# Four weight block sums formed during the first feed-forward product and kept in DRAM

## The chip, the cores and the metric

The kernel runs on one core of a Trainium2 chip. The metric is the time of one execution in microseconds (us), measured on the device. Five engines of the core matter: TensorE (PE in the profile) multiplies; VectorE (DVE), ScalarE (ACT) and GpSimd (POOL) work elementwise; SyncE (SP) issues nearly all DMA transfers, in the order in which its program lists them, and stands still where it waits for a semaphore.

## The reference, cut to what matters

The reference is two transformer blocks over 512 tokens of width 1024, all in float32. The change touches only the end of the second block:

```python
def hybrid_layer(x, ...):
    ...
    h = rms_norm_2(x, norm_mlp)
    return x + jnp.square(jax.nn.relu(h @ w_ff1)) @ w_ff2   # w_ff1 1024x4096, w_ff2 4096x1024

def second_block(x, ...):
    ...
    return rms_norm_2(x, norm_final)
```

## The kernel before

Every float32 matrix is split into a high part (the value rounded to `fp32r`) and a low part (value minus high part), and a product is three matmuls: high by high, low by high, high by low. ACT writes the high parts, DVE subtracts to get the low parts, and PE adds the three into one PSUM bank.

**First feed-forward product** (`ff_tile`). 32 output chunks `c` of 128 features by 512 tokens. A chunk takes 8 x 3 = 24 matmuls of 128x512. Its weights (`unit`, 128x1024) come from a ring `wring` whose slots hold four chunks each (groups `f1_0` to `f1_7`, 2048 KB per group). ACT copies the unit to `w_hi` (L1652) once PE is done with chunk `c - 3`, DVE makes `w_lo` (L2214), ACT applies relu and square into `ffT` (L1350, L1352). SP refills a slot once DVE has made the four low parts of its last group (`last_use`, L609). The ring has three slots.

**Second feed-forward product.** The 4096 rows of `w_ff2` are taken as 16 pairs of 128 rows. A pair is a 2x2 block matrix (two row blocks by two column halves of 512; in `pair_raw` they lie as quarters 0 to 3), and the activations of the pair are 2x2 as well (two chunks by two halves of the tokens). The kernel uses a seven-product scheme in place of eight: each product is a block or sum of blocks of the activations by a block or sum of blocks of the weights. All seven do not fit in the eight PSUM banks, so there are two sweeps over the 16 pairs: indices m = 0 to 15 form four products per pair (`first_of`, 24 matmuls), m = 16 to 31 three (`second_of`, 18 matmuls, the weights loaded a second time). Between the sweeps DVE adds the eight banks into `x` while PE works on the last two pairs.

For each m the steps are: SP loads 1024 KB of `w_ff2` into one of six places (L742; place m is free when pair m - 6 has been used by PE, semaphore `pair_used`); POOL forms the weight sums in place (`weight_sums`: L2424, 1024 wide, and L2426, 512 wide, in the first sweep; L2428 and L2429, 512 wide each, in the second), and in the first sweep one sum of activations (`side_sum`, L2418, 256 wide); DVE forms two differences of activations in the first sweep (L2236, 512 wide); ACT writes `s_hi` (L1675) and `f_hi` (L1682 to L1686); DVE writes `s_lo` (L2240, 2048 wide, in the second sweep 1536) and `f_lo` (L2243 and L2244, 256 and 768 wide; in the second sweep L2246 and L2247, 256 and 512). PE waits for `f_lo_done` before each pair. The high and low activations have four places; places 1 to 3 lie where the high and low parts of the first product's input are, so `side_sum(1)` waits until that product has ended (`a_full`, `A2_END + NF`). During the first feed-forward product POOL also adds two totals per pair to `ffT` (`side_totals`, L2409 and L2410).

At the end the last four pairs are held: product 0 of all four is finished first, then the others bank by bank, so that the final norm of the first token tiles runs beside PE.

## Time and profile before

| | us |
|---|---|
| three timed runs | 1111.55, 1111.72, 1116.86 (median 1111.72) |
| profiled execution | 1115.25 |
| its span, first to last instruction | 1113.4 |
| PE busy | 1055.2 (95%) |
| DVE busy | 696.2 (63%) |
| ACT busy | 513.8 (46%) |
| POOL busy | 316.6 (28%) |
| DMA | 121 MB, mean 109 GB/s |

Busy time is a share of the whole span and hides that the stages have different limits: the strip of the page with 40 slices shows PE at 9 tenths or more nearly everywhere up to the 32nd slice (28 us each), and 6 to 8 tenths in most of the slices after that, where the second feed-forward product runs. Matmul durations overlap in the records: a 128x512 matmul is shown as about 0.39 us and the next one starts 0.23 us after it. The granted clock says at which share of 2.4 GHz PE ran.

### The profile page before, as it was taken

The page shows a single profiled execution, that of the slowest core. Times are in us where ns is not written, and L with a number is a line of the kernel's source. Part 1 is how long each engine was busy: PE and PEld are TensorE (multiplying, and loading weights), DVE is VectorE, ACT ScalarE, POOL GpSimd, SP SyncE. Part 2 cuts the span into 40 slices and gives each one's busy share as a digit, 9 for nine tenths or more (in the row PEclk, how much of TensorE's full clock was granted, in tenths as well). Part 3 has the DMA queues.
Part 4 walks back from the last instruction along what each step waited for, and adds up shares of the span by engine and source line. Part 5 has one row for each costly group of instructions (what it writes and reads, how often), then busy time and mean ns, then how long its engine had stood idle before and what let it go on. Part 6 is the DMA issues. An engine that isn't in the chain of part 4 may idle for free. (4 is left out here: it accounts for less than half of the span.)

```text
span 1113.4 us, 14191 instructions
## 1 busy us (share of the span) xinstructions
PE 1055.2 (95%) x5364; PEld 856.9 (77%) x5364; DVE 696.2 (63%) x1156; ACT 513.8 (46%) x929; POOL 316.6 (28%) x274
## 2 busy tenths in 40 slices
PE   9999999999899999999999999999999967887896
PEld 7788888888788889877777778888888855666664
DVE  5579996666853335154678693422222389999896
ACT  8453454554642422454678642343333433444543
POOL 0021110022300018001444100011111689874971
PEclk9999999999999999999999999999999988998999
DMA  8554332324100852222004511433223213342752
GB/s 314 109 120 114 95 89 63 77 95 152 68 29 21 271 170 58 76 76 53 5 1 151 190 45 70 151 134 113 76 76 117 110 43 128 131 151 94 257 178 76
DMA packets 79283, 121.06 MB, mean 109 GB/s; under 512 B 4288, under 2 KB 41920, under 8 KB 79216
## 3 DMA queue, kind: packets, MB, share of 16 engines
q1 hardware_dynamic: 78288, 117.37, 32.5%
q0 software_dynamic: 784, 2.75, 1.7%
q8 instruction: 43, 0.70, 0.3%
q14 instruction: 24, 0.20, 0.1%
q10 hardware_dynamic: 144, 0.03, 0.0%
HBM read 115.30 MB, written 4.85 MB: 108 GB/s over the span
## 5 line engine op out<-in xcount | busy, mean ns | idle before, releaser
L1228 PE MATMUL bank<-s_hi,f_hi 128*128 128x512 f32 x224 | 95.3, 426 | 39.1 <-DVE f_lo L2244 30.4
L2214 DVE TENSOR_TENSOR w_lo<-wring,w_hi 128x1024 fp32r<-128x1024 f32 x32 | 40.6, 1267 | 122.5 <-ACT w_hi L1652 122.5
L784 PE MATMUL bank<-u_hi,h_hi 128*128 128x512 f32 (+1 forms) x288 | 110.9, 385 | 1.4 <-ACT arena L1321 1.1
L1782 DVE TENSOR_TENSOR u_lo<-wring,u_hi 128x1024 fp32r<-128x1024 f32 (+1 forms) x64 | 78.9, 1242 | 53.3 <-ACT u_hi L1394 52.7
L784 PE MATMUL bank<-u_hi,h_lo 128*128 128x512 f32 (+1 forms) x288 | 109.2, 379 | 0.0
L784 PE MATMUL bank<-u_lo,h_hi 128*128 128x512 f32 (+1 forms) x288 | 109.0, 378 | 0.0
L1394 ACT ACTIVATE u_hi<-wring 128x1024 fp32r<-128x1024 f32 (+1 forms) x64 | 65.9, 1034 | 87.0 <-PE bank L784 68.1
L784 PE MATMUL bank<-h_hi,w_lo 128*128 128x512 f32 (+2 forms) x272 | 104.5, 384 | 0.0
L784 PE MATMUL bank<-h_hi,w_hi 128*128 128x512 f32 (+2 forms) x272 | 104.4, 384 | 0.0
L784 PE MATMUL bank<-h_lo,w_hi 128*128 128x512 f32 (+2 forms) x272 | 104.3, 384 | 0.0
L784 PE MATMUL bank<-h_hi,u_hi 128*128 128x512 f32 x224 | 95.1, 424 | 0.3 <-ACT arena L1336 0.2
L1230 PE MATMUL bank<-s_lo,f_hi 128*128 128x512 f32 x224 | 92.0, 411 | 0.0
L1229 PE MATMUL bank<-s_hi,f_lo 128*128 128x512 f32 x224 | 91.9, 410 | 0.0
L2240 DVE TENSOR_TENSOR s_lo<-wring,s_hi 128x2048 fp32r<-128x2048 f32 (+1 forms) x32 | 84.6, 2645 | 9.2 <-ACT s_hi L1675 9.2
L1228 PEld LDWEIGHTS bank<-s_hi,f_hi 128*128 128x128 f32 x224 | 44.5, 199 | 59.1 <-DVE f_lo L2244 35.9
L784 PE MATMUL bank<-h_hi,u_lo 128*128 128x512 f32 x224 | 87.9, 392 | 0.0
L784 PE MATMUL bank<-h_lo,u_hi 128*128 128x512 f32 x224 | 87.6, 391 | 0.0
L2409 POOL TENSOR_TENSOR arena<-arena 128x256 f32<-128x256 f32 x16 | 11.8, 737 | 244.1 <-ACT arena L1352 244.1
L1652 ACT ACTIVATE w_hi<-wring 128x1024 fp32r<-128x1024 f32 x32 | 33.9, 1058 | 95.4 <-PE bank L784 95.4
L2395 POOL TENSOR_SCALAR arena<-arena,stats 128x128 f32<-128x128 f32 (+3 forms) x64 | 39.4, 626 | 123.7 <-DVE stats L2167 123.7
L1675 ACT ACTIVATE s_hi<-wring 128x2048 fp32r<-128x2048 f32 (+1 forms) x32 | 54.2, 1693 | 37.2 <-PE bank L1230 26.2
L784 PEld LDWEIGHTS bank<-u_hi,h_hi 128*128 128x128 f32 x288 | 54.1, 188 | 13.0 <-issue 2.9
(322 smaller groups left out, 2532.4 us busy)
## 6 DMA issues: line engine op xcount, KB each, us to landing
wring<-in_w_ff SPq DMA_DIRECT2D x32, 1024.0 KB, 4.9
wring<-in_w_in SPq DMA_DIRECT2D x60, 512.0 KB, 3.9
wring<-in_w_ff SPq DMA_DIRECT2D x8, 2048.0 KB, 8.2
arena<-in_w_out SPq DMA_DIRECT2D x4, 1024.0 KB, 5.1
wring<-in_w_out SPq DMA_DIRECT2D x2, 2048.0 KB, 12.5
arena<-in_first SPq DMA_DIRECT2D x8, 418.0 KB, 5.6
arena<-in_x SPq DMA_DIRECT2D x4, 512.0 KB, 10.5
arena<-bias_copies POOLq DMA_DIRECT2D x8, 256.0 KB, 5.9
```

The lines of the kernel that those rows point to most:

```text
L784: last = mm(b, lhs, rhs, start=(start and n == 0), stop=(stop and n == 2))
L1228: mm(b, f[0][:, token], w[0][:, high], start=start, stop=False)
L1229: mm(b, f[1][:, token], w[0][:, high], start=False, stop=False)
L1230: return mm(b, f[0][:, token], w[1][:, lows], start=False, stop=stop)
L1394: run(u_hi[u % HI_UNITS][:, 0:unit_cols(u)], raw_unit(u), ACT.Copy).then_inc(u_hi_done, 1)
L1652: run(dst, src, ACT.Copy).then_inc(w_hi_done, 1)
L1675: run(s_hi[m % 4][:, 0:PAIR - at], pair_raw(m)[:, at:PAIR], ACT.Copy).then_inc(s_hi_done, 1)
L1782: v.tensor_tensor(u_lo[u % RAW_UNITS][:, 0:cols], raw_unit(u), u_hi[u % HI_UNITS][:, 0:cols].bitcast(F32), ALU.subtract).then_inc(u_lo_don ...
L2214: v.tensor_tensor(cut(w_lo[ring3(m)]), src, cut(w_hi[ring3(m)]).bitcast(F32), ALU.subtract).then_inc(w_lo_done, 1)
L2240: v.tensor_tensor(s_lo[pair_place(m)][:, at:PAIR], pair_raw(m)[:, at:PAIR], s_hi[m % 4][:, 0:PAIR - at].bitcast(F32), ALU.subtract)
L2395: g.tensor_scalar(place, place, den2[:, u:u + 1], gates[:, i, at:at + 1], ALU.mult, ALU.mult).then_inc(scaled, 1)
L2409: g.tensor_tensor(f[:, 256:512], f[:, 256:512], f[:, 768:D], ALU.add)
```

## The change

1. **POOL and SP during the first product.** While PE runs the first feed-forward product, each pair of `w_ff2` is loaded into one of two places in the middle slot of the ring (`load_pair`), POOL forms four of the five weight sums (`pair_sums`: one instruction 1024 wide, two 512 wide), and SP writes them to a DRAM tensor `sums_kept` (`keep_sums`, two transfers of 512 KB). The next load into the place waits until that write has landed. The first-product groups `f1_2` to `f1_7` now alternate between two slots only, and their loads stand in SP's program behind rounds 0, 3, 6, 9, 12 and 14 of this loop.
2. **First sweep.** SP loads two quarters of `w_ff2` and one kept sum (three transfers of 256 KB); POOL adds one sum of 512 (`weight_sum`) and one activation sum of 256.
3. **Second sweep.** SP loads three kept sums (768 KB). POOL forms no weight sum; it forms one sum and one difference of activations, 256 wide each.
4. **Products regrouped.** The four products of the first sweep take one difference of activations from DVE (256 wide, `side_diff`) in place of two. `f_lo` is made by two instructions of 512. The adds into `x` between the sweeps are 14 in place of 12, those at the end 10 in place of 12; behind the very last product stands one add and one square in place of two and two.
5. **A place for pair 1** (index m = 1): its activations go to `wring` 0 to 2047, which is also place 0 of the weight ring. `side_sum(1)` waits for `w_lo_done` 32 in place of the end of the first product. The load for m = 4, which uses that same place, waits for `pair_used` 2. In DVE's program `side_diff(m + 1)` now stands ahead of `lows(m)`.

```diff
+    sums_kept = nc.dram_tensor("sums_kept", (NP, P, PAIR), F32).ap()
...
+        f_at = (("arena", 26720), ("hT", 0), ("hT", 2 * D), ("arena", 24672), ("wring", 0))
+        f_place = lambda m: 4 if m == 1 else m % 4
+        sum_raw = lambda j: wring[:, SLOT + PAIR * (j % 2):SLOT + PAIR * (j % 2 + 1)]
+        sum_out = [wring[:, 12288:12288 + D], arena[:, 26720:26720 + D]]
...
         def slot(name, width=512):
-            s = number[name] % RING
+            s = (2, 0)[int(name[3:]) % 2] if name[0] == "f" else number[name] % RING
...
+            def load_pair(j):
+                if j < 2:
+                    sp.wait_ge(*last_use("w2o1"))
+                else:
+                    sp.wait_ge(sums_out, 32 * (j - 1))
+                rows = w["w_ff2_2"][2 * P * j:2 * P * (j + 1), :]
+                sp.dma_start(sum_raw(j).rearrange("p (k n) -> p k n", k=2), rows.rearrange("(k p) n -> p k n", p=P)).then_inc(piece_in[6 + j % 2], 16)
+
+            def keep_sums(j):
+                sp.wait_ge(w_summed, 3 * j + 3)
+                sp.dma_start(sums_kept[j][:, 0:D], sum_out[j % 2]).then_inc(sums_out, 16)
+                sp.dma_start(sums_kept[j][:, D:PAIR], sum_raw(j)[:, S:S + D]).then_inc(sums_out, 16)
...
+            for j in range(NP):
+                keep_sums(j)
+                if j + 2 < NP:
+                    load_pair(j + 2)
+                if j in (0, 3, 6, 9, 12, 14):
+                    n = 2 + (0, 3, 6, 9, 12, 14).index(j)
+                    sp.wait_ge(w_lo_done, 4 * (n - 1))
...
+            sp.wait_ge(sums_out, 32 * NP)
             for m in range(2 * NP):
-                if m < PAIR_PLACES:
+                if 2 <= m < PAIR_PLACES:
                     sp.wait_ge(w_lo_done, 4 * (6 + m // 2))
+                if m == 4:
+                    sp.wait_ge(pair_used, 2)
+                if m >= PAIR_PLACES:
+                    sp.wait_ge(pair_used, m - PAIR_PLACES + 1)
...
+            def side_diff(m):
+                dve.wait_ge(side_sum_done, m + 1)
+                total = f_sum[f_place(m)]
+                v.tensor_tensor(total[:, 768:D], ff_pair(m)[:, 256:512], total[:, 512:768], ALU.subtract).then_inc(side_diff_done, 1)
...
-            for m in range(NP + 2):
+            side_diff(0)
+            side_diff(1)
+            lows(0)
+            lows(1)
+            side_diff(2)
+            for m in range(2, NP + 2):
+                if m + 1 < NP:
+                    side_diff(m + 1)
                 lows(m)
...
+            def pair_sums(j):
+                pool.wait_ge(piece_in[6 + j % 2], 16 * (j // 2 + 2))
+                raw = sum_raw(j).rearrange("p (q n) -> p q n", q=4)
+                g.tensor_tensor(sum_out[j % 2].rearrange("p (q n) -> p q n", q=2), raw[:, 1:3, :], raw[:, 0:4:3, :], ALU.add).then_inc(w_summed, 1)
+                pool.wait_ge(w_summed, 3 * j + 1)
+                g.tensor_tensor(raw[:, 1, :], raw[:, 1, :], raw[:, 3, :], ALU.subtract).then_inc(w_summed, 1)
+                g.tensor_tensor(raw[:, 2, :], raw[:, 2, :], raw[:, 0, :], ALU.subtract).then_inc(w_summed, 1)
+
+            def weight_sum(m):
+                pair_arrived(pool, m)
+                raw = pair_raw(m)
+                g.tensor_tensor(raw[:, 3 * S:PAIR], raw[:, 0:S], raw[:, S:2 * S], ALU.add).then_inc(w_summed, 1)
...
             def side_sum(m):
-                if m >= 4:
+                if m == 1:
+                    pool.wait_ge(w_lo_done, NF)
+                elif m >= 4:
                     pool.wait_ge(pair_used, m - 3)
...
+            for m in range(4, NP):
+                weight_sum(m)
+                side_sum(m)
+            for m in range(NP, 2 * NP):
+                side_sum(m)
```

SP's program around the two feed-forward products, before (`in_w_ff_2 128x8x512` is a group of `w_ff1`, `128x2x1024` a pair of `w_ff2`):

```order
L653 DMA wring<-in_w_branch_pool 128x4x128
L697 DMA wring<-in_w_ff_2 128x8x512 x4
L735 DMA arena<-in_norm_final 128x1024
L697 DMA wring<-in_w_ff_2 128x8x512 x4
L742 DMA wring<-in_w_ff_2 128x2x1024 x32
```

The same place in the changed program (rounds 0 to 2 of the 16):

```order
L702 DMA wring<-in_w_ff_2 128x8x512 x2
L745 DMA wring<-in_w_ff_2 128x2x1024 x2
L749 DMA sums_kept<-wring 128x1024
L750 DMA sums_kept<-wring 128x1024
L745 DMA wring<-in_w_ff_2 128x2x1024
L762 DMA wring<-in_w_ff_2 128x8x512
L749 DMA sums_kept<-arena 128x1024
L750 DMA sums_kept<-wring 128x1024
L745 DMA wring<-in_w_ff_2 128x2x1024
L749 DMA sums_kept<-wring 128x1024
L750 DMA sums_kept<-wring 128x1024
L745 DMA wring<-in_w_ff_2 128x2x1024
```

Each round is two writes and one load (L749, L750, L745). The load of group `f1_2` (L762), which followed straight on `f1_1` before, now stands behind the writes of round 0 and the load for pair 2; `f1_3` stands at the same place of round 3.

DVE's program near the start of the second product, before, for m = 2 (`s_lo4`) and m = 3 (`s_lo5`), four instructions for each:

```order
L2236 TENSOR_TENSOR hT<-arena,hT 128x512 [waits side_sum_done]
L2240 TENSOR_TENSOR s_lo4_134<-wring,s_hi2_128 128x2048 [waits s_hi_done]
L2243 TENSOR_TENSOR f_lo2_142<-arena,f_hi2_138 128x256 [waits f_hi_done]
L2244 TENSOR_TENSOR f_lo2_142<-hT,f_hi2_138 128x768
L2236 TENSOR_TENSOR arena<-arena 128x512 [waits side_sum_done]
L2240 TENSOR_TENSOR s_lo5_135<-wring,s_hi3_129 128x2048 [waits s_hi_done]
L2243 TENSOR_TENSOR f_lo3_143<-arena,f_hi3_139 128x256 [waits f_hi_done]
L2244 TENSOR_TENSOR f_lo3_143<-arena,f_hi3_139 128x768
```

The same place in the changed program:

```order
L2280 TENSOR_TENSOR hT<-arena,hT 128x256 [waits side_sum_done]
L2280 TENSOR_TENSOR arena<-arena 128x256 [waits side_sum_done]
L2287 TENSOR_TENSOR s_lo4_134<-wring,s_hi2_128 128x2048 [waits s_hi_done]
L2290 TENSOR_TENSOR f_lo2_143<-arena,f_hi2_138 128x512 [waits f_hi_done]
L2291 TENSOR_TENSOR f_lo2_143<-hT,f_hi2_138 128x512
L2280 TENSOR_TENSOR wring<-arena,wring 128x256 [waits side_sum_done]
L2287 TENSOR_TENSOR s_lo5_135<-wring,s_hi3_129 128x2048 [waits s_hi_done]
L2290 TENSOR_TENSOR f_lo3_144<-arena,f_hi3_139 128x512 [waits f_hi_done]
L2291 TENSOR_TENSOR f_lo3_144<-arena,f_hi3_139 128x512
```

The difference for m = 3 (L2280, the second row) stands ahead of the low parts for m = 2, and the one for m = 4 (`wring<-arena,wring`, the sixth row) ahead of those for m = 3; each waits for POOL's activation sum of its own m.

POOL's program at the same place, before, for m = 2 to 5 (`piece_in4` says that the pair m = 2 has landed, `piece_in0` m = 4):

```order
L2424 TENSOR_TENSOR wring<-wring 128x1024 [waits piece_in4]
L2426 TENSOR_TENSOR wring<-wring 128x512 [waits w_summed]
L2409 TENSOR_TENSOR arena<-arena 128x256 [waits a_free]
L2410 TENSOR_TENSOR arena<-arena 128x256
L2418 TENSOR_TENSOR hT<-arena 128x256 [waits a_full]
L2424 TENSOR_TENSOR wring<-wring 128x1024 [waits piece_in5]
L2426 TENSOR_TENSOR wring<-wring 128x512 [waits w_summed]
L2418 TENSOR_TENSOR hT<-arena 128x256 [waits a_full]
L2424 TENSOR_TENSOR wring<-wring 128x1024 [waits piece_in0]
L2426 TENSOR_TENSOR wring<-wring 128x512 [waits w_summed]
L2418 TENSOR_TENSOR arena<-arena 128x256 [waits a_full]
L2424 TENSOR_TENSOR wring<-wring 128x1024 [waits piece_in1]
```

And in the changed program (L2475 is `weight_sum`, L2486 `side_sum`):

```order
L2475 TENSOR_TENSOR wring<-wring 128x512 [waits piece_in4]
L2475 TENSOR_TENSOR wring<-wring 128x512 [waits piece_in5]
L2486 TENSOR_TENSOR hT<-arena 128x256 [waits a_full]
L2461 TENSOR_TENSOR arena<-arena 128x256 [waits a_free]
L2462 TENSOR_TENSOR arena<-arena 128x256
L2486 TENSOR_TENSOR arena<-arena 128x256 [waits a_full]
L2475 TENSOR_TENSOR wring<-wring 128x512 [waits piece_in0]
L2486 TENSOR_TENSOR wring<-arena 128x256 [waits pair_used]
L2475 TENSOR_TENSOR wring<-wring 128x512 [waits piece_in1]
L2486 TENSOR_TENSOR hT<-arena 128x256 [waits pair_used]
```

The activation sum for m = 4 (`waits pair_used`, eighth row) stands behind the weight sum for m = 4, which waits for the load of that pair (`piece_in0`).

## Rows read from the trace of the kernel before

**Rows 1.** Windows: per stretch, busy us (instructions) of each engine, clock, DMA share, GB/s.

```profile
727.00:894.00 167.00, 167.00 (x725) 135.13 (x725) 43.31 (x33) 68.69 (x93) 36.03 (x37) 1.00 0.29 104
894.00:1018.00 124.00, 93.63 (x350) 71.32 (x349) 119.42 (x61) 48.20 (x52) 101.37 (x51) 0.88 0.36 119
1018.00:1106.00 88.00, 79.24 (x329) 60.65 (x327) 79.68 (x77) 38.55 (x59) 50.40 (x27) 1.00 0.43 150
```

**Rows 2.** Waits of PE from 892 to 1107: us in total, times, longest.

```profile
PE bank L1228 <- DVE f_lo L2244: 30.4, 12, 8.0
PE bank L1228 <- DVE f_lo L2247: 8.8, 10, 1.4
```

**Rows 3.** One source line, L1228: duration ns, first and last start in us.

```profile
L1228 PE MATMUL bank<-s_hi,f_hi x224: 389/397/797, 894.9 to 1105.4; 128*128 128x512 f32 x112
```

**Rows 4.** Timeline of PE within one pair: start us, us, engine, line.

```profile
1003.45 0.39 PE L1229 MATMUL bank<-s_hi,f_lo 128*128 128x512 f32 x1
...
1008.57 0.40 PE L1230 MATMUL bank<-s_lo,f_hi 128*128 128x512 f32 x1
```

**Rows 5.** Timeline of DVE over one pair beside POOL and one alone.

```profile
984.96 2.28 DVE L2240 TENSOR_TENSOR s_lo<-wring,s_hi 128x2048 fp32r<-128x2048 f32 x1
...
992.82 2.28 DVE L2240 TENSOR_TENSOR s_lo<-wring,s_hi 128x2048 fp32r<-128x2048 f32 x1
995.02 0.41 DVE L2243 TENSOR_TENSOR f_lo<-arena,f_hi 128x256 fp32r<-128x256 f32 x1
995.36 0.94 DVE L2244 TENSOR_TENSOR f_lo<-wring,f_hi 128x768 fp32r<-128x768 f32 x1
996.23 0.68 DVE L2236 TENSOR_TENSOR hT<-arena,hT 128x512 f32<-128x512 f32 x1
996.83 3.38 DVE L2240 TENSOR_TENSOR s_lo<-wring,s_hi 128x2048 fp32r<-128x2048 f32 x1
```

**Rows 6.** Timeline of POOL: three instructions with DVE idle, then those beside the pair.

```profile
864.71 0.73 POOL L2410 TENSOR_TENSOR arena<-arena 128x256 f32<-128x256 f32 x1
865.40 2.40 POOL L2424 TENSOR_TENSOR wring<-wring 128x1024 f32<-128x1024 f32 x1
867.88 1.30 POOL L2426 TENSOR_TENSOR wring<-wring 128x512 f32<-128x512 f32 x1
...
985.91 3.58 POOL L2424 TENSOR_TENSOR wring<-wring 128x1024 f32<-128x1024 f32 x1 [1.43 <-DMA wring<-in_w_ff]
989.57 1.36 POOL L2426 TENSOR_TENSOR wring<-wring 128x512 f32<-128x512 f32 x1
991.43 0.92 POOL L2418 TENSOR_TENSOR hT<-arena 128x256 f32<-128x256 f32 x1 [0.49 <-PE bank L1230]
```

**Rows 7.** Timeline of DVE in the first feed-forward product, two chunks in a row.

```profile
751.39 1.23 DVE L2214 TENSOR_TENSOR w_lo<-wring,w_hi 128x1024 fp32r<-128x1024 f32 x1 [4.41 <-ACT w_hi L1652]
756.89 1.23 DVE L2214 TENSOR_TENSOR w_lo<-wring,w_hi 128x1024 fp32r<-128x1024 f32 x1 [4.28 <-ACT w_hi L1652]
```

**Rows 8.** Timeline of SP: the loads of groups `f1_1` and `f1_2` (x2, merged).

```profile
706.87 6.82 SPq L697 DMA_DIRECT2D wring<-in_w_ff  x2
```

**Rows 9.** Landing of the two 1024 KB loads issued at 836.2 and 836.6.

```profile
L742 SPq DMA_DIRECT2D wring<-in_w_ff x2: 367/418/469, 836.2 to 836.6; - x2
DMA to landing us min/median/max: 4.7/5.8/6.8
```

**Rows 10.** Page, DMA issues: the writes of the output, 256 KB each.

```profile
out<-x SPq DMA_DIRECT2D x8, 256.0 KB, 2.0
```

**Rows 11.** Windows around DMA transfers and around PE's longest wait, columns as in rows 1.

```profile
836.00:844.00 8.00, 8.00 (x36) 6.49 (x35) 1.35 (x2) 2.19 (x4) 1.43 (x2) 1.00 0.71 262
1107.00:1113.00 6.00, 0.00 (x0) 0.00 (x0) 2.28 (x5) 2.19 (x7) 2.49 (x2) 0.82 0.58 219
...
907.00:910.00 3.00, 1.35 (x3) 1.16 (x4) 3.00 (x2) 0.00 (x0) 2.92 (x3) 0.50 0.00 0
910.00:913.00 3.00, 3.00 (x9) 2.28 (x8) 3.00 (x3) 2.63 (x3) 3.00 (x2) 0.52 0.00 0
```

**Rows 12.** Chain that ended last, its end: start us, us, what.

```profile
1106.27 1.29 DVE x L2254 x2
1107.56 0.02 issue
1107.58 0.94 ACT junk L1706 x3
```

## What was predicted

> **What bounds the kernel now.** I read the windows by stage first, then the waits of PE, then PE, DVE and POOL on the timeline, and the transfers last. In the first feed-forward product PE is busy in all of 727 to 894, while DVE works 43 of 167 us, POOL 36 and the DMA engines 0.29 of the time [rows 1]. In the second product, 894 to 1106, it is the other way round: DVE is busy 119.4 of 124 us in the first sweep and 79.7 of 88 in the rest, POOL 101 and 50, and PE has gaps [rows 1]. All of PE's waits there are for DVE's last instruction of a pair, `f_lo`, 39.2 us in 22 waits, the longest 8.0 [rows 2]. The granted clock is 0.88 in the first of the two stretches [rows 1]: the gaps also cost speed behind them.
>
> What PE would need: from the second to the last matmul of a pair, 22 steps, 5.12 us pass, 0.2327 us a matmul [rows 4]. A first-sweep pair of 24 is 5.58 us, a second-sweep pair of 18 is 4.19, and all 3 x 224 = 672 [rows 3] are 156.4 us. They took from 894.9 to 1106.2 [rows 3, 12], 211.3 us. So 54.9 us lie between this stage and a dense PE.
>
> What DVE needs: alone it starts the instructions of a pair 2.20 (2048 wide), 0.34 (256), 0.87 (768) and 0.60 us (512) apart, 4.01 us for the four (992.82 to 996.83) [rows 5]. One pair earlier, beside POOL, the same four took 992.82 - 984.96 = 7.86 us [rows 5]. In that time POOL did three instructions that alone take 2.48, 1.26 and 0.70 us, 4.44 in sum [rows 6] (865.40 to the next start, 867.88, and 0.03 to 0.04 less than the shown length for the other two). The extra 3.85 us is 0.87 of POOL's own work. So a pair costs DVE its own time plus 0.87 times what POOL does meanwhile: 4.01 + 0.87 x 4.44 = 7.9 us against PE's 5.58. DVE is the bound of the sweeps, and POOL's work is half the reason.
>
> **The sweeps, part by part.** First sweep, POOL per pair: the 1024-wide sum goes, 512 and 256 wide stay, 1.96 us in place of 4.44. DVE: 2.20 + one difference of 256 (0.34) + 2 x 0.60 = 3.74 in place of 4.01. Together 3.74 + 0.87 x 1.96 = 5.45 us, just under PE's 5.58. Second sweep: POOL has 2 x 0.70 = 1.40 in place of two sums of 512 (2.52); DVE is unchanged, an estimate of 1.65 for the 1536-wide low part (three quarters of 2.20) + 0.34 + 0.60 = 2.6. Together 3.8 us against PE's 4.19 (before: 4.8). In both sweeps PE becomes the bound, by a hair in the first.
>
> Here a rule speaks against the change. The Trainium skill (SBUF — State Buffer, "SBUF: two separate sides") says that DVE and GpSimd share a port pair under an exclusive lock, held for the whole instruction, the other side fully blocked. By it the two simply add up, 3.74 + 1.96 = 5.70 us, and the first sweep stays DVE-bound by 0.12 us a pair, 2 us in all. This trace has them a little better than additive: 4.01 + 4.44 = 8.45 by the rule, 7.86 measured [rows 5, 6].
>
> What PE then still loses. (a) m = 3. Pair 1 now lies in `wring` 0 to 2047, so the load for m = 4 is issued when PE has used pair 1, 2 x 5.58 = 11.2 us into the sweep (m = 0 and 1 can both be ready at its start: the activations of m = 1 no longer wait for the end of the first product, which was the 8.0 us wait). In POOL's program the activation sum of m = 4 stands behind the weight sum of m = 4, and in DVE's the difference of m = 4 stands ahead of the low parts of m = 3. So the chain is: issue 11.2; 768 KB land after 3/4 of 2.85 (below) + 1.6 + 0.5 for three issues = 4.2, 15.4; POOL 1.26 + 0.70, 17.4; DVE 0.34 + 2.20 + 1.20, 21.1; beside it POOL does the sums of m = 5, + 0.87 x 1.96 = 22.8. PE wants m = 3 at 16.7. A stall of 6.1 us. Nothing else queues long behind it: m = 4 follows 5.45 later. (b) The clock behind it. After the 8.0 us gap PE started at 908.65 and ran at half clock until about 912.9 (1.35 us busy of 907 to 910, clock 0.52 in 910 to 913) [rows 11], 2.1 us lost; I take 2. (c) Where DVE has 0.1 us of slack per pair, hiccups remain: bounds 0 and 0.4 us for each of the 16 pairs, I take 4 us for this, the sweep boundary (DVE adds 14 x 0.6 = 8.4 us there, PE has two pairs = 8.4 us in hand) and the four held pairs. Sum: 156.4 + 6.1 + 2 + 4 = 168.5 us in place of 211.3: **-42.8**.
>
> **Tail.** Behind the last product stood two adds (1.29 us) and two squares (0.94 us shown to the second's start of reading) [rows 12]; one add and one square stay: -0.6 and about -0.5. **-1.1**.
>
> **The first product: the new work.** POOL gets 16 x (2.48 + 2 x 1.26) = 80 us on an engine that has 131 idle [rows 1]; DVE's `w_lo` may take 1 us longer each, and has 4.3 us of idle ahead of it [rows 7]. Both are hidden. The DMA queue is another matter. 1024 KB move in 2.85 us (0.71 of 8 us for 2048 KB), written at the same rate (0.58 of 6 us at 219 GB/s, which is 1.31 MB) [rows 11]; two loads issued 0.4 us apart landed 4.7 and 6.8 us after their issues, that is one after the other, with 7.2 - 5.7 = 1.5, I take 1.6 us beside the moving [rows 9]. SP does one round per pair: write the sums, wait until they have landed, load the pair after next, next round. The write of a round stands behind the load of the one before, so a round is 2.85 + 2.85 + 1.6 + 0.3 for semaphores = 7.6 us (POOL's 5.0 + 1.4 fit in). Every third round also has a `w_ff1` group in front of the write, + 5.7 = 13.3. Three rounds are 28.5 us, with the write waiting a little for POOL 28.8. PE eats a group of four chunks in 4 x 24 x 0.2327 = 22.3 us [rows 4] (one chunk from 751.39 to 756.89 [rows 7]). Supply is slower than use, the ring is one slot shorter, and what counts is how long the head start lasts:
> - the first pair loads are issued at 713.3 (706.87 + 6.82 - 0.37) [rows 8], land 718, summed 723.5, written 728, then load and group: `f1_2` is there at 739.5;
> - `f1_6` is four triples later, 739.5 + 115.2 = 854.7. Its first chunk (24) starts in PE eight chunks, 8 x 5.58 = 44.6 us, before the end of the product (894.4, half a microsecond ahead of the first start in [rows 3]), at 849.8, and ACT and DVE need 2.4 us: wanted at 847.4. **7.3 us late**. `f1_5` is 0.8 late, `f1_7` (two rounds later) arrives at 871, wanted at 869.7 + 7.3, in time. So PE waits at chunks 20 and 24, 7.3 us together, and about 1.5 us of half clock behind: **+8.8**.
> The loads of the sweeps start when all sums are out, about 874, and m = 0 is wanted near the end of the product: hidden.
>
> The Trainium skill (DMA: Bandwidth & Descriptors, "Anatomy of one DMA") puts a fixed 2.0 us on a transfer, most of it the receipt of the last write, longest where the target is HBM, and every round here waits for just that. The output writes give 2.0 - 0.7 = 1.3 us for it [rows 10, 11]. With the page's 2.0 a round would be 0.4 us longer, 12 rounds lie before `f1_6`, and the sum would be 4.8 us higher.
>
> **The sum.** -42.8 - 1.1 + 8.8 = -35.1 us, against the profiled execution of 1115.25 (span 1113.4 and 1.85 around it): 1080.2. That execution lies 3.5 us above the median of the timed runs; I carry the difference over and forecast 1111.7 - 35.1 = **1077 us**.
>
> **The rivals.**
> - *The rounds keep up.* If a group may overtake or the fixed part is nearer 1.3, `f1_6` comes in time and the first product stays whole: 8.8 less, 1068. For it: PE's slack is only missed by 7 in 115 us. Against it: it needs all triples at 27 us or less.
> - *Longer rounds.* One microsecond more per round (POOL slowed by DVE, a slower receipt, the write not right behind the load) comes 12 times: 1089. For it: a chain of waits across SP, DMA and POOL seldom runs without gaps; before, such a wait of SP did not exist in this stage.
> - *The rounds starve the first product* (the other side). Place: PE at chunks 16, 20 and 24, waiting for `w_hi`. The saving of 43.9 is eaten when `f1_6` is 44 us late less the clock, which is 12 rounds of 10.6 in place of 7.6 and up: writes to DRAM at less than half the rate of reads. With 3.5 us more per round, 1119. Against it: the output writes move at the rate of reads [rows 11].
> - *DVE stays the bound.* If what an instruction of DVE loses is a fixed 1.1 us (3.38 against 2.28 [rows 5]) whenever POOL is active at all, not a share of POOL's work, a first-sweep pair costs 3.74 + 4 x 1.1 = 8.1 and the sweep gains nothing: 1077 + 16 x 2.5 = 1117 and more. Against it: POOL will be idle two thirds of each pair, and the pair at 992.82 shows no loss while POOL idles.
>
> **Chances.** Forecast, 1072 to 1083: 0.47. Rounds keep up, 1064 to 1072: 0.20. Longer rounds or larger rests in the sweeps, 1083 to 1102: 0.24. The two last: 0.03 and 0.02, and 0.04 for something in between that leaves no change. Faster 0.91, same 0.04, slower 0.05, where within 0.5% (5.6 us) a measurement can't tell a change from none. Range 1060 to 1099: both ends reach past the neighbouring cases, since the length of a round enters twelvefold.
>
> **What would show it.** In the windows of the changed kernel: DVE's share in the first sweep still near 1 but a pair in 5.6 us; PE's waits for `f_lo` down from 39 to about 10, of them one of 6 us at m = 3, 16 to 17 us into the sweep; writes of sums spaced 7.6 and 13.3 us; two waits of PE on `w_lo` at chunks 20 and 24, 1 and 6.5 us; POOL near 116 us busy in the first product. The forecast is wrong if PE waits in the first product at chunk 16 already or not at all, or if DVE takes over 6 us a pair in the first sweep.

## The result: 1.5% faster, less than half of the forecast gain

| | before | changed |
|---|---|---|
| median of 4 timed runs each, us | 1112.84 | 1096.54 (1095.39 to 1097.95) |
| ratio | | 0.985, 95% interval 0.982 to 0.988 |
| span of the profiled execution, us | 1113.4 | 1096.1 |
| second product: first and last start of its first line | 894.9, 1105.4 | 920.3, 1088.1 |

16.3 us were gained where 35.1 were forecast. The second product is as short as forecast; it begins 25.4 us later than before, where 8.8 were forecast.

Windows of the changed kernel, the first product and then the second, columns as in [rows 1]:

```profile
727.00:920.00 193.00, 176.47 (x735) 141.61 (x735) 51.77 (x35) 70.17 (x97) 113.12 (x81) 0.95 0.71 244
920.00:1089.00 169.00, 159.78 (x675) 127.81 (x673) 136.85 (x140) 89.18 (x112) 67.78 (x62) 0.97 0.39 134
```

PE now has 16.5 us of gaps in the first product, which was gapless [rows 1], and POOL works 113 us there in place of 36 (over 193 us in place of 167). In the second, DVE is busy 81% of the stretch; in [rows 1] it was 94% over the two. PE's waits from 700 to 1097 (total, times, longest), and the line that answers to [rows 3]:

```profile
PE bank L826 <- ACT arena L1394: 16.5, 3, 6.0
PE bank L1270 <- DVE f_lo L2291: 9.0, 1, 9.0
...
L1270 PE MATMUL bank<-s_hi,f_hi x224: 389/396/792, 920.3 to 1088.1; 128*128 128x512 f32 x112
```

Of the 22 waits for `f_lo` [rows 2] one is left. The 16.5 us are new, and they are not waits for `w_lo` but for ACT's square (L1394), which releases a PSUM bank.

SP's timeline over one triple of rounds, that is three rounds of which the first has a group in front of its writes (L745 loads a pair, L749 and L750 write its sums, L762 loads a group of `w_ff1`):

```profile
728.24 0.38 SPq L745 DMA_DIRECT2D wring<-in_w_ff  x1
728.67 0.52 SPq L762 DMA_DIRECT2D wring<-in_w_ff  x1
731.07 0.34 SPq L749 DMA_DIRECT2D sums_kept<-arena  x1
...
741.57 0.38 SPq L745 DMA_DIRECT2D wring<-in_w_ff  x1
...
751.75 0.38 SPq L745 DMA_DIRECT2D wring<-in_w_ff  x1
...
760.19 0.38 SPq L745 DMA_DIRECT2D wring<-in_w_ff  x1
760.62 0.47 SPq L762 DMA_DIRECT2D wring<-in_w_ff  x1
```

Rounds of 13.3, 10.2 and 8.4 us, where 13.3, 7.6 and 7.6 were forecast. The next groups are issued at 792.4, 824.0, 855.2 and 869.5: over the four triples 31.6 us each and not 28.8. Windows show the rate, first over a round with a group (three quarters of its bytes are reads) and then in stretches of three such triples where a load and a write follow each other alone:

```profile
728.50:741.50 13.00, 13.00 (x59) 10.58 (x58) 4.05 (x4) 5.90 (x8) 8.34 (x5) 1.00 0.89 323
742.00:748.00 6.00, 6.00 (x28) 4.84 (x27) 1.49 (x2) 2.33 (x4) 0.01 (x1) 1.00 0.81 242
774.00:780.00 6.00, 6.00 (x28) 4.84 (x27) 1.23 (x1) 2.66 (x5) 1.06 (x1) 1.00 0.86 249
805.90:812.00 6.10, 6.10 (x16) 4.76 (x17) 1.23 (x1) 1.83 (x3) 0.00 (x0) 0.55 0.77 207
```

Divided by the share of time in which the DMA engines were busy: 323 / 0.89 = 363 GB/s in the first, then 299, 290 and 269. [rows 11] gave 262 / 0.71 = 369 for reads alone and 219 / 0.58 = 378 for writes alone: neither shows the two together.

ACT's timeline where `f1_6` lands, then the SP line L762 as a whole, who waits for it and how long its transfers take:

```profile
865.55 1.06 ACT L1694 ACTIVATE w_hi<-wring 128x1024 fp32r<-128x1024 f32 x1 [12.59 <-DMA wring<-in_w_ff]
866.51 0.58 ACT L1392 ACTIVATE arena<-bank 128x512 f32<-128x512 f32 x1
867.12 0.63 ACT L1394 ACTIVATE arena<-arena 128x512 f32<-128x512 f32 x1
```

```profile
L762 SPq DMA_DIRECT2D wring<-in_w_ff x6: 469/471/870, 728.7 to 869.5; - x6
...
  ACT w_hi L1694: 36.4, 3
DMA to landing us min/median/max: 10.3/10.7/13.8
```

In ACT's program the copy of chunk c + 3 (L1694) stands ahead of the relu and square of chunk c (L1392, L1394). When a group is late, ACT stands at its first unit (chunk c + 3), and the bank of chunk c, which PE has finished, stays full. PE has two banks for this product, so it can still work on c + 1 and is stopped before c + 2: one chunk, 5.58 us, before it would need the late weights.

### The profile page after: what moved, and what is told of

It is laid out like the page before. It is cut to its first block and busy times, and to the rows that moved or that the text cites. A ratio compares the mean times of both kernels' runs of the same rounds, so it can differ in the third digit from the quotient of the medians.

```text
span 1096.1 us, 14319 instructions
## 1 busy us (share of the span) xinstructions
PE 1051.2 (96%) x5364; PEld 858.7 (78%) x5364; DVE 644.7 (59%) x1156; ACT 515.6 (47%) x929; POOL 318.2 (29%) x306
## 5 line engine op out<-in xcount | busy, mean ns | idle before, releaser
L2261 DVE TENSOR_TENSOR w_lo<-wring,w_hi 128x1024 fp32r<-128x1024 f32 x32 | 48.4, 1513 | 137.1 <-ACT w_hi L1694 137.1
L826 PE MATMUL bank<-h_hi,w_hi 128*128 128x512 f32 (+2 forms) x272 | 108.0, 397 | 16.9 <-ACT arena L1394 16.5
L826 PE MATMUL bank<-h_lo,w_hi 128*128 128x512 f32 (+2 forms) x272 | 107.2, 394 | 0.0
L826 PE MATMUL bank<-h_hi,w_lo 128*128 128x512 f32 (+2 forms) x272 | 107.1, 394 | 0.0
L1270 PE MATMUL bank<-s_hi,f_hi 128*128 128x512 f32 x224 | 89.7, 400 | 9.1 <-DVE f_lo L2291 9.0
L1694 ACT ACTIVATE w_hi<-wring 128x1024 fp32r<-128x1024 f32 x32 | 33.8, 1057 | 121.0 <-PE bank L826 84.6
L1271 PE MATMUL bank<-s_hi,f_lo 128*128 128x512 f32 x224 | 89.5, 400 | 0.0
L1272 PE MATMUL bank<-s_lo,f_hi 128*128 128x512 f32 x224 | 89.0, 398 | 0.0
L2287 DVE TENSOR_TENSOR s_lo<-wring,s_hi 128x2048 fp32r<-128x2048 f32 (+1 forms) x32 | 68.5, 2141 | 14.3 <-ACT s_hi L1720 14.3
L826 PEld LDWEIGHTS bank<-h_hi,w_hi 128*128 128x128 f32 x272 | 53.0, 195 | 29.6 <-ACT arena L1394 17.8
L826 PEld LDWEIGHTS bank<-u_lo,h_hi 128*128 128x128 f32 x288 | 54.1, 188 | 10.1
```

Source lines behind the costliest of these rows:

```text
L826: last = mm(b, lhs, rhs, start=(start and n == 0), stop=(stop and n == 2))
L1270: mm(b, f[0][:, token], w[0][:, high], start=start, stop=False)
L1271: mm(b, f[1][:, token], w[0][:, high], start=False, stop=False)
L1272: return mm(b, f[0][:, token], w[1][:, lows], start=False, stop=stop)
L1694: run(dst, src, ACT.Copy).then_inc(w_hi_done, 1)
L2261: v.tensor_tensor(cut(w_lo[ring3(m)]), src, cut(w_hi[ring3(m)]).bitcast(F32), ALU.subtract).then_inc(w_lo_done, 1)
```

## The experiments

The ratios of e1 to e12 are to runs of the kernel before on the chip of that experiment, medians 1114.7 to 1115.7 us; the ratio of the changed kernel is to the 1112.8 us of the first table. Spans and starts are of one execution each. "Start" and "last" are the first and last start of the second product's first line (`bank<-s_hi,f_hi`, x224) in the profiled execution.

| kernel | start | last | difference | span | median | ratio (95%) |
|---|---|---|---|---|---|---|
| changed | 920.3 | 1088.1 | 167.8 | 1096.1 | 1096.5 | 0.985 (0.982 to 0.988) |
| e1_takefirst | 911.9 | 1078.3 | 166.4 | 1086.4 | 1088.5 | 0.977 (0.975 to 0.980) |
| e2_early | 908.3 | 1076.3 | 168.0 | 1084.4 | 1086.9 | 0.976 (0.974 to 0.979) |
| e3_sidefirst | 920.2 | 1085.4 | 165.2 | 1093.5 | 1093.6 | 0.981 (0.979 to 0.983) |
| e4_reads | 913.2 | 1078.9 | 165.7 | 1086.9 | 1087.5 | 0.976 (0.973 to 0.978) |
| e5_place5 | 919.7 | 1076.5 | 156.8 | 1084.6 | 1085.7 | 0.974 (0.972 to 0.976) |
| e6_joined | 902.8 | 1064.8 | 162.0 | 1072.8 | 1075.1 | 0.964 (0.963 to 0.966) |
| e7_double | 916.6 | 1091.6 | 175.0 | 1099.1 | 1103.1 | 0.990 (0.987 to 0.992) |
| e8_oldplace | 919.7 | 1079.1 | 159.4 | 1087.2 | 1088.3 | 0.976 (0.974 to 0.978) |
| e9_split | 913.2 | 1080.9 | 167.7 | 1089.0 | 1091.3 | 0.979 (0.975 to 0.982) |
| e10_all | 901.1 | 1064.1 | 163.0 | 1072.2 | 1070.3 | 0.960 (0.957 to 0.964) |
| e11_all2 | 895.7 | 1057.1 | 161.4 | 1065.2 | 1068.6 | 0.960 (0.957 to 0.962) |
| e12_split2 | 912.5 | 1079.0 | 166.5 | 1087.1 | 1088.8 | 0.977 (0.975 to 0.980) |

**ACT's order (e1_takefirst).**

```diff
+                take(("ff", c))
                 if c + 3 < NF:
                     unit_hi(c + 3)
-                take(("ff", c))
```

> ScalarE's order in the first product is turned round: take(c) (relu and square of chunk c) stands ahead of unit_hi(c + 3), the copy that waits for the group from DMA. Theory A, the deadline: in the changed kernel ScalarE stands at unit_hi(4n) waiting for the group, take(4n - 3) stands behind it, and PE finds no free bank for chunk 4n - 1, so the group is wanted one chunk (5.58 us) earlier than its weights are used. Then PE's waits become waits for w_lo, and the second product starts 5.6 us earlier (914.7 in place of 920.3), the time falls by 5 to 6 us. Rival: the lateness is only that of the group against its first use; then turning the order changes nothing (within 1 us).

Its waits of PE, 700 to 1100:

```profile
PE bank L826 <- DVE w_lo L2261: 12.6, 2, 6.6
```

Three waits for ACT have become two for `w_lo`, the releaser and the number that the prediction had, at 6.0 and 6.6 us and not 1 and 6.5. The second product starts 8.4 us sooner, more than the 5.6 expected: `f1_6` was also issued 2.2 us sooner here (853.0 against 855.2). The span is 9.7 us shorter, since the sweeps took 1.4 us less as well. The prediction had put the deadline of a group one chunk too late.

How far a start moves by itself: e3, e5, e7 and e8 leave the loads, POOL's sums and PE's matmuls of the first product as in the changed kernel and start at 920.2, 919.7, 916.6 and 919.7. So a difference of under 4 us between two starts shows nothing by itself.

**The groups sooner (e2_early).**

```diff
-                if j in (0, 3, 6, 9, 12, 14):
+                if j in (0, 2, 4, 6, 8, 10):
```

> The groups f1_2 to f1_7 are loaded behind rounds 0, 2, 4, 6, 8 and 10 in place of 0, 3, 6, 9, 12 and 14; everything else as in the changed kernel. If the whole stretch of the first product (25.4 us) is the supply of the groups, PE is dense there again, the second product starts at 894 to 896, and what is late next is the round of pair 15: the sums are still out at about 886, the loads for m = 0 land at 891, and PE waits 3 to 8 us for its first pair. Time lower by 18 to 22 us. Rival: the DMA queue is full anyway, groups that come earlier push the writes back, the sums end later (895 or more) and half of the gain goes: 8 to 12 us.

PE no longer waits for weights in the first product, yet the second starts only 12 us earlier. PE's wait and DVE's timeline there:

```profile
908.35 0.77 PE L1270 MATMUL bank<-s_hi,f_hi 128*128 128x512 f32 x1 [12.41 <-DVE f_lo L2291]
```

```profile
896.91 0.43 DVE L2280 TENSOR_TENSOR wring<-arena,wring 128x256 f32<-128x256 f32 x1 [14.27 <-POOL wring L2486]
901.19 0.94 DVE L2280 TENSOR_TENSOR wring<-arena,wring 128x256 f32<-128x256 f32 x1 [3.85 <-POOL wring L2486]
902.05 2.81 DVE L2287 TENSOR_TENSOR s_lo<-wring,s_hi 128x2048 fp32r<-128x2048 f32 x1
```

The loads of the sweeps start when the last sums have landed, 889.0 here (885.8 in the changed kernel). The wait for weights had covered a second one, for the sums. The 11.7 us of span lie in the range of the rival (8 to 12) and not in the 18 to 22 expected: PE is dense as expected, the sums end 3 us later, not 10, and the wait for the first pair is 12.4 us, not 3 to 8. The difference for m = 1, which waits 3.85 us for POOL, stands ahead of the low parts of m = 0 and adds to it.

**Reads in place of writes (e4_reads).**

```diff
-                sp.dma_start(sums_kept[j][:, 0:D], sum_out[j % 2]).then_inc(sums_out, 16)
+                sp.dma_start(sum_out[j % 2], w["w_ff2_2"][2 * P * j:2 * P * j + P, :]).then_inc(sums_out, 16)
```

> The two writes of sums to DRAM per round are replaced by two loads of the same size (512 KB each) from w_ff2 into the same places of SBUF, and the loads of kept sums in the sweeps by loads of w_ff2 of the same size: same bytes, same order, same waits, but no DMA write to DRAM (the products then use other weights). Theory B, mixed directions: reads and writes in one queue together move at about 290 GB/s where reads alone move at 350, so a triple of rounds takes 31.6 us in place of 28.8; then without writes the triple is 28 to 29 us and the time falls by 9 to 12 us. Rival C, latency: the rounds are long because of fixed parts of waiting and issuing; then the triple stays at 31 to 32 us and the time stays within 2 us.

The second write of a round is replaced in the same way, and in the sweeps the loads of kept sums are loads of `w_ff2` of the same size; the kernel leaves out the keeping of the sums and multiplies by other weights.

The groups are issued at 728.6, 758.1, 788.9, 818.8 and 848.0: 29.85 us a triple. So 1.75 of the 2.8 us that a triple was too long belong to the writing to DRAM. The time met its number (9.2 us of span, 9 to 12 expected), the triple did not (28 to 29 expected): a part of the excess has another cause. A window of it beside that of 742 to 748 above:

```profile
743.00:749.00 6.00, 6.00 (x28) 4.84 (x27) 1.23 (x1) 2.18 (x3) 1.81 (x1) 1.00 0.82 329
```

329 / 0.82 = 401 GB/s against 299, with a load in the place of each write. The edit takes away two things at once, the slower moving and the landing of a write in DRAM. The end of this round, where the last bytes have moved and SP still waits, in the changed kernel and then in e4:

```profile
750.00:752.00 2.00, 2.00 (x10) 1.64 (x9) 0.00 (x0) 0.85 (x1) 1.92 (x3) 1.00 0.04 16
748.00:750.00 2.00, 2.00 (x10) 1.64 (x9) 0.00 (x0) 0.00 (x0) 1.92 (x2) 1.00 0.04 14
```

The DMA engines stand still for about as long in both (the next load is issued at 751.75 and 749.63), so in this round it is the moving that got longer; other rounds were not compared in this way.

**Place and order in the sweeps (e3_sidefirst, e5_place5, e8_oldplace).** e3 puts POOL's activation sum of m = 4 ahead of its weight sum; e5 moves pair 1 to place 1, so that the load for m = 5 waits and not that for m = 4, and puts the activation sums of 4 and 5 first; e8 undoes the place for pair 1, in all engines' programs, and puts `lows(0)` ahead of `side_diff(1)` in DVE's.

```diff
 # e3
-            for m in range(4, NP):
-                weight_sum(m)
-                side_sum(m)
+            side_sum(4)
+            weight_sum(4)
 # e5
-        ..., ("wring", 0))
+        ..., ("wring", PAIR))
-                if m == 4:
+                if m == 5:
 # e8
-        f_place = lambda m: 4 if m == 1 else m % 4
+        f_place = lambda m: m % 4
```

> On GpSimd the activation sum for m = 4 stands ahead of the weight sum for m = 4, which waits for the load. If the 9.0 us wait at m = 3 is the chain load, weight sum, activation sum, difference, low parts (as read from the program), it goes whole: PE's only wait for f_lo vanishes or shrinks below 1 us, with it the half clock behind it (about 2.5 us): 10 to 12 us less. Rival: the low parts of m = 3 are late because DVE has too much to do beside GpSimd at the start of the sweep; then the wait moves to m = 4 and 3 us or less are won.

> Turning POOL's order for m = 4 alone moved PE's wait of 9.0 us from m = 3 to m = 4 (6.2 us). Here the activations of pair 1 lie in place 1 of the weight ring (wring 2048 to 4095) in place of place 0, so the load for m = 4 no longer waits for pair_used 2 and the one for m = 5 does, and on GpSimd the activation sums for m = 4 and 5 stand ahead of the weight sums. If the chain from the late load is all there is, both waits go: no wait for f_lo over 1 us in the first sweep, the span 11 to 12 us below the changed kernel's 1096.1. Rival: the wait moves once more, to m = 5, and 4 us or less are won.

> The place for pair 1 is undone: its activations lie at the end of the first product's input as before, side_sum(1) waits for the end of that product, the load for m = 4 waits for nothing in the sweep; on DVE the low parts of m = 0 stand ahead of the difference for m = 1, so that they don't wait for it. If the place was needed, PE waits 3 us or more for m = 1 and the time stays within 3 us of the changed kernel. If, as the timeline of the sweep's start suggests, the chain of m = 1 (sum 0.7, difference 0.4, high parts 1.2, low parts 1.2 us) fits into the 5.58 us of pair 0, then no wait at all is left in the first sweep and the span falls by 11 to 12 us: the place cost more than it gave.

PE's waits from 900 on, in e3, e5 and e8:

```profile
PE bank L1270 <- DVE f_lo L2291: 6.2, 1, 6.2
```

```profile
PE bank L1270 <- DVE f_lo L2291: 0.4, 1, 0.4
```

```profile
PE bank L1268 <- DVE f_lo L2288: 2.8, 2, 1.5
```

e3 missed: the wait moved from m = 3 to m = 4, and 2.6 us were gained where 10 to 12 were expected. By its place and size this is what the rival said, but not by its reason, too much work on DVE: DVE stands 10 us still there, for the difference of m = 5, whose activation sum on POOL stands behind a weight sum that waits for its load (e3, POOL and DVE):

```profile
940.28 1.30 POOL L2475 TENSOR_TENSOR wring<-wring 128x512 f32<-128x512 f32 x1 [0.80 <-DMA wring<-sums_kept]
941.54 0.74 POOL L2486 TENSOR_TENSOR hT<-arena 128x256 f32<-128x256 f32 x1
942.31 0.42 DVE L2280 TENSOR_TENSOR hT<-arena,hT 128x256 f32<-128x256 f32 x1 [10.01 <-POOL hT L2486]
```

e5 met its number (11.5 us), and PE's sweeps are all but gapless: 156.8 us between the two starts. e8 gained 8.9 us, not 11 to 12; 2.8 us of waits remain. With e8 the part "place for pair 1" is measured, together with the order of `lows(0)`: the two cost the changed kernel 9 us (span 1096.1 against 1087.2). That it is nearly all the place is argued and was not run by itself: the starts are alike (920.3 and 919.7), and the 8.4 us lie behind them, where the wait of 9.0 us at m = 3 is gone.

**How DVE pays for POOL (e7_double).**

```diff
+                if m >= 6:
+                    g.tensor_tensor(raw[:, 3 * S:PAIR], raw[:, 0:S], raw[:, S:2 * S], ALU.add).then_inc(pool_chain, 1)
+                    pool.wait_ge(pool_chain, chain[0] + m - 5)
```

> GpSimd does its 512-wide weight sum twice for m = 6 to 15 of the first sweep, result unchanged: 1.26 us more of its work per pair. Theory of the prediction: DVE's pair costs its own 3.74 us plus 0.87 times GpSimd's work, 3.74 + 0.87 x 3.22 = 6.54 against PE's 5.58, less the slack that DVE has built up (it runs up to one pair ahead): 10 pairs x 0.96 - 3 = 6 to 8 us slower, PE waits for f_lo at most of these pairs. Rule of the exclusive lock, both add up: 6.96, 10 x 1.38 - 3 = 10 to 12 us. Rival: the sweeps are dense because PE is far from the bound; then nothing changes (within 1.5 us).

DVE's timeline over one pair, from the end of `f_lo` to the end of the next:

```profile
974.64 0.68 DVE L2291 TENSOR_TENSOR f_lo<-wring,f_hi 128x512 fp32r<-128x512 f32 x1
...
975.24 0.95 DVE L2280 TENSOR_TENSOR hT<-arena,hT 128x256 f32<-128x256 f32 x1
...
976.11 3.38 DVE L2287 TENSOR_TENSOR s_lo<-wring,s_hi 128x2048 fp32r<-128x2048 f32 x1
...
979.41 1.77 DVE L2290 TENSOR_TENSOR f_lo<-arena,f_hi 128x512 fp32r<-128x512 f32 x1
...
981.11 0.68 DVE L2291 TENSOR_TENSOR f_lo<-hT,f_hi 128x512 fp32r<-128x512 f32 x1
```

A pair takes 981.11 - 974.64 = 6.47 us. By the prediction's 0.87 it is 3.74 + 0.87 x (0.70 + 2 x 1.26) = 6.54, by full addition 6.96. The share holds a second time, at another mix (here (6.47 - 3.74) / 3.22 = 0.85). The second product became 7.2 us longer, where the share asked for 6 to 8 and the full addition for 10 to 12.

**Three edits joined (e6_joined):** e5, e2 and e1, and `lows(0)` ahead of `side_diff(1)` in DVE's program.

> Everything found so far together: groups of w_ff1 behind rounds 0, 2, 4, 6, 8, 10; ScalarE takes a chunk ahead of the copy that waits for DMA; pair 1 in place 1 with the activation sums for m = 4 and 5 first; and on DVE the low parts of m = 0 stand ahead of the difference for m = 1. With the early groups alone PE's first pair of the sweep waited 12.4 us for f_lo (start 908.3 against 894.9 in the kernel before). The order on DVE should bring it 6 us forward (it stood behind the activation sum of m = 1, 901.2, while its high parts were ready at 898.2), and the wait at m = 3 goes. Expected span: 1084.4 - 6 - 11 = 1067, the time near 1070. If the end of the sums (889) governs more than that order does, 1073 to 1076.

The rival came out, with 1072.8 us of span and 1075.1 of time where it said 1073 to 1076: the last sums are issued at 884.2, the sweeps' loads at 888.1, and PE waits 7.5 us at 902.8.

**A pair's load cut in two (e9_split, e10_all), the first two pairs whole again (e11_all2, e12_split2).** e9 is the changed kernel with this edit alone, e10 is e6 with it; e12 and e11 are the same two with whole loads for j < 2.

```diff
             for j in range(NP):
                 keep_sums(j)
                 if j + 2 < NP:
+                    load_blocks(j + 2, (0, 3))
                     load_pair(j + 2)      # now only blocks 1 and 2, behind the wait for the writes
```

> The changed kernel with one edit: a pair's load in the rounds is cut into four blocks of 256 KB. The two outer blocks, whose place is free as soon as GpSimd has read them, are queued right behind the round's writes; only the two middle ones, into which the sums are written back, wait until the writes have landed. Theory A (the length of a round is the failed term, and it is set by SyncE's chain write, receipt, load, write on one queue): half a load, 1.4 us at the rate of reads and up to 2 at the mixed rate, moves into the time of the receipt, in each of the 12 rounds before f1_6; a round without a group goes from 9 or 10 to about 8, where GpSimd's own 7.4 to 8.4 us a pair (757.75 to 766.18 to 773.5) take over; a triple goes from 31.6 to about 28, f1_6 lands 12 to 16 us earlier, PE's waits in the first product fall from 25.5 to about 10, and the span from 1096 to about 1083. Theory B (GpSimd, slowed by VectorE in its own sums, sets the rounds already): triples stay at 31 and more, the span at 1094 to 1096. Theory C (the engines' moving alone sets them, so that any order of the same bytes takes the same time, and smaller pieces a little more): triples 31.6 to 33, span 1096 to 1100.

> The four edits that helped and do not exclude each other, in one kernel: pair 1 in place 1 with GpSimd's activation sums of m = 4 and 5 first, the f1 loads behind rounds 0, 2, ..., 10, ScalarE's release of the bank ahead of its wait for the next group, VectorE's low parts of m = 0 ahead of the difference of m = 1, and the load of a pair cut into outer and middle blocks. Without the last edit the second product began at 902.8, 7.5 us late, since the last sums went out at 884.6. Theory A: with shorter rounds they go out by 872 to 876, the second product begins at the end of the first, 895 to 896, and the waits of the sweeps fall from 10.5 to about 2: span 1062 to 1065, time 1064 to 1067. Theory B or C (rounds no shorter): 1072 to 1075.

> e10_all with the loads of pairs 0 and 1 whole again (one transfer each); from pair 2 on they stay cut. In e10_all PE waited 1.41 us for h_lo at 723.7 (0.25 with whole loads) and ran at a clock of 0.69, 0.50 and 0.96 in 724 to 742; the first product ended at 901 in place of 894.9. Theory A (that stall is the cause: GpSimd's first sums stood beside both of VectorE's h_lo, 4.50 us in place of 3.33, and the clock fell behind it): the clock stays at full in 724 to 742, all that follows lies 6 us earlier, the last sums go out at about 876, the second product begins at 895 to 896, span 1064 to 1067, time 4 to 7 us under that of e10_all. Theory B (the smaller transfers, or the supply by them, slow the first product otherwise): the clock still falls, or the second product begins at 900 and later; time as e10_all, within 2 us.

> e9_split with the loads of pairs 0 and 1 whole again: the changed kernel with the one edit that from pair 2 on a pair's load is cut into outer and middle blocks. In e9_split a triple of rounds fell from 31.6 to 29.3 us, but the clock fell in 724 to 736 as well. Theory A (as for e11_all2): full clock there. PE then uses the weights some 5 us sooner than in e9_split, the supply is as before, so PE's waits at chunks 20 and 24 grow by part of it, and the second product begins 1 to 5 us earlier than its 913.2: span 1084 to 1088. Theory B: as e9_split, within 1 us, low clock included.

Triples fell to 29.3 us in e9 and 29.7 in e12 (groups issued from 731.3 to 848.4 and from 729.4 to 848.3), not to 28; the span of e9 to 1089.0 where 1083 was expected. e12's span lies where it was expected, at 1087.1, with full clock in 724 to 736 and its waits in the first product at 12.4 us in place of 8.0; its start, 912.5, is only 0.7 us sooner than e9's. e10 missed its 1062 to 1065 by 7 us and lies at 1072, where its rivals "rounds no shorter" had it: its groups go out from 730.6 to 844.0, e6's from 729.4 to 842.4, its last sums at 882.3, not 872 to 876, and the clock fell at the start of the first product. e11, with the same cut from pair 2 on, has its groups from 730.0 to 838.5, so the cut does shorten the rounds where the clock stays. Windows of e10 from 718 to 736, PE's wait in them, and the windows of e11 from 724 on:

```profile
718.00:724.00 6.00, 4.59 (x28) 4.27 (x27) 5.90 (x5) 2.18 (x3) 4.91 (x3) 1.00 0.47 171
724.00:730.00 6.00, 6.00 (x41) 6.00 (x39) 2.83 (x2) 2.18 (x3) 5.92 (x4) 0.69 0.72 245
730.00:736.00 6.00, 6.00 (x19) 5.07 (x19) 1.73 (x2) 2.17 (x3) 3.31 (x2) 0.50 0.81 280
```

```profile
723.70 0.33 PE L833 MATMUL bank<-h_hi,w_hi 128*128 128x128 f32 x1 [1.41 <-DVE h_lo L1859]
```

```profile
724.00:730.00 6.00, 6.00 (x49) 5.73 (x49) 2.92 (x2) 3.45 (x6) 5.92 (x4) 1.00 0.77 258
730.00:736.00 6.00, 6.00 (x28) 4.86 (x27) 1.23 (x1) 2.57 (x4) 2.62 (x2) 1.00 0.95 303
```

The share of PE in 724 to 736 is full in both, but at 60 and 77 matmuls. At that place POOL's first sums run beside both of DVE's `h_lo`, which take 4.50 us in e10 and 3.56 in e11. With whole first loads the wait is 0.5 us, the clock stays, the last sums are issued at 876.5 in place of 882.3, and the second product starts at 895.7, at the end of a gapless first one. The profiled spans differ by 7.0 us as expected (5 to 8), the medians only by 1.6 (expected 4 to 7): e10's four runs are 1067.8, 1068.3, 1072.2 and 1074.0 at mean granted clocks of 0.997, 0.996, 0.995 and 0.992 (e11: 0.995 to 0.998), so the fall of the clock seems to be in only some of them; only the last was traced. e10 and e11 are the best versions, 45 and 46 us faster than the kernel before, and 27 to 28 us faster than the changed one by their ratios; they can't be told apart.

## Why the prediction was wrong

The step that failed is the term for the first product, forecast at 8.8 us and measured at 25.4: the length of a round, and the time at which a group is wanted. The other terms of the sum came out at -42.8 (as forecast) and 0 (-1.1 forecast).

- **What bounds the sweeps: right.** DVE with POOL's work in its price. A first-sweep pair takes 5.55 us (957.26 to 962.81 for two `s_lo`), PE's own pace, of which DVE stands 0.63 still:

```profile
957.26 2.28 DVE L2287 TENSOR_TENSOR s_lo<-wring,s_hi 128x2048 fp32r<-128x2048 f32 x1
959.46 0.68 DVE L2290 TENSOR_TENSOR f_lo<-arena,f_hi 128x512 fp32r<-128x512 f32 x1
960.07 0.68 DVE L2291 TENSOR_TENSOR f_lo<-hT,f_hi 128x512 fp32r<-128x512 f32 x1
961.38 1.50 DVE L2280 TENSOR_TENSOR wring<-arena,wring 128x256 f32<-128x256 f32 x1 [0.63 <-POOL wring L2486]
962.81 2.28 DVE L2287 TENSOR_TENSOR s_lo<-wring,s_hi 128x2048 fp32r<-128x2048 f32 x1
```

  4.92 us of work where 5.45 were forecast, since POOL's activation sum falls largely into DVE's pause. By the rule of the Trainium skill (SBUF — State Buffer, "SBUF: two separate sides") the prediction had a pair of 5.70 us; the measured pair is shorter, but with a pause in it it is no test of the rule. e7 is one, without a pause: 6.96 us by the rule, 6.47 measured. From the first start of the second product to the end of its last matmul 168.5 us pass: the forecast's 168.5. That the number is met is luck, since its parts were other ones: the stall at m = 3 was 9.0 and not 6.1 us, 2.6 us of low clock followed and not 2, and the 4 us for rests were hardly used.
- **The stall at m = 3: right in place and chain.** The load for m = 4 is issued at 931.77, 11.5 us into the sweep (11.2 forecast). From there (SP, POOL, DVE and PE rows of the timeline):

```profile
931.77 0.33 SPq L777 DMA_DIRECT2D wring<-in_w_ff  x1
...
937.77 1.26 POOL L2475 TENSOR_TENSOR wring<-wring 128x512 f32<-128x512 f32 x1 [13.48 <-DMA wring<-sums_kept]
...
938.99 0.73 POOL L2486 TENSOR_TENSOR wring<-arena 128x256 f32<-128x256 f32 x1
...
940.09 3.36 DVE L2287 TENSOR_TENSOR s_lo<-wring,s_hi 128x2048 fp32r<-128x2048 f32 x1
...
946.30 0.79 PE L1270 MATMUL bank<-s_hi,f_hi 128*128 128x512 f32 x1 [9.02 <-DVE f_lo L2291]
```

  The load took 6.0 us, not 4.2 (the loads for m = 5 to 7, which stand behind it in SP's program, followed right on it; that they slowed it was not tested). DVE, from its difference at 939.74 to the end of `f_lo`, took 6.4 us beside POOL (forecast 5.4). e5 and e8 show what the prediction did not ask: the stall is the price of this place in this order of the programs, and another place with POOL's sums turned round (e5), or none (e8), is 9 to 12 us better.
- **Tail: not seen.** From the start of the last matmul to the end of the span 7.6 us pass, as before. The add and the square went, and DVE's last pass started 2.4 us behind that matmul's start in place of 3.6; but it took 1.96 us for its two instructions in place of 1.42, beside POOL, and the output writes behind it ended another 0.7 us later. Of 1.1 us nothing was left.
- **The first product: here it failed.** The step "a round is 7.6 us, three rounds 28.8" and the step "wanted at 847.4". The first took the rate of reads and the rate of writes, each measured alone (369 and 378 GB/s), for the rate of both together (269 to 299); a triple took 31.6 us, and `f1_6` landed at 865.5 and not 854.7, 10.8 us later. Over the four triples the rounds with a group took 13.3 to 14.0 us (13.3 forecast), those without one 7.4 to 10.2, 9.0 in the mean (7.6 forecast): most of the excess is in the latter. e4 gives 1.75 of the 2.8 us a triple to the writes; the other 1.05 were not taken apart and stay open. In the third round of the first four triples SP waits 0.9, 0.9, 1.9 and 3.2 us for POOL's sums, where the prediction had 0.3 a triple; the load in front of the write is still moving then, so what these waits cost is not shown. The fixed 2.0 us that the prediction set beside its sum (the Trainium skill, DMA: Bandwidth & Descriptors, "Anatomy of one DMA") is given there for transfers issued by GpSimd, while these are issued by SP. With it the sum would have been 4.8 us higher and still short. That the order within a round counts too, e9 and e12 show: half a load queued during the receipt gives back 2 us a triple. The second overlooked that ACT's release of the bank stands behind its wait for the group, which puts the deadline one chunk, 5.6 us, earlier (e1: the waits for ACT are gone, the start 8.4 us sooner, 2.2 of them from an earlier load). 10.8 + 5.6 = 16.4 of the 16.6 us by which this term was off (25.4 in place of 8.8). PE waited for `f1_4` already, 4.5 us ahead of chunk 15 (until 805.7), and the prediction had named a wait at chunk 16 as the sign that it is wrong.
- **The rivals.** "Longer rounds", one microsecond each, is what happened (0.9 us a round), at 0.24; it priced the sum at 1089 where 1096.5 were measured, because it shared the late deadline. Starving the first product did not come, nor a DVE bound.

## What to carry to other kernels

Price a chain of transfers by a stretch that has the same mix of reads and writes, or widen the range for it; an error in one round counts twelvefold here. Find the deadline of a buffer from the order of every engine that handles it: an engine that waits for late data in front of a release stops its neighbour sooner than the data are needed. And when a first limit is lifted, ask which one stood right behind it: in e2 the end of the sums, hidden until then, kept 13.4 of the 25.4 us by which the second product was late.

## What the runs showed of the hardware

- Reads and writes in flight together on one queue moved at 269 to 299 GB/s of busy time where both were 1024 KB, at 363 where reads were three quarters of the bytes; reads alone at 369 [rows 11] to 401 (e4), writes alone at 378 [rows 11].
- A wait of PE of 1.41 us at the start of a stage, where its matmuls are 128 wide, was followed by 12 us at granted clocks of 0.69 and 0.50, with no further wait (e10; e9 fell in the same way after 1.39 us, to 0.64 and 0.51). In the changed kernel, e11 and e12 the wait there was 0.35, 0.47 and 0.82 us, and the clock stayed at 1.00. What else may differ just before was not separated: PE is busy 4.59 us of 718 to 724 in e10 and 5.53 in e11.
- DVE's 256-wide difference takes 0.42 us alone, 0.95 or 1.50 beside POOL; a 512-wide `f_lo` 0.68 or 1.77; the 2048-wide `s_lo` 2.28 or 3.38: losses near 0.55 or 1.1 us in these rows, whatever the width. Over a whole pair the loss was 0.85 of POOL's own work in e7 and 0.87 in [rows 5, 6].
